# Weight sums of a seven-product scheme: three of four moved from VectorE to accumulating transfers issued by GpSimd

## The reference

```
xn   = rms_norm(h);  proj = xn @ w_in
h    = h + concat(gated_deltanet(...), moba_attention(...)) @ w_o
hn   = rms_norm(h)
h    = h + (silu(hn @ w_gate) * (hn @ w_up)) @ w_down        # w_gate, w_up: 2048 x 5632
gate = sigmoid(rms_norm(h) @ w_ple_gate)                     # 2048 x 2048
h    = h + gate * (p @ w_ple_proj)
```

## Time and profile before

| | |
|---|---|
| median of three runs | 1308.66 us (1308.38 to 1309.03) |
| span of the profiled execution, from its first to its last instruction | 1306.8 us |
| median of the runs above that span | 1.9 us |
| TensorE busy | 1299.9 us (99%) |
| VectorE busy | 1041.3 us (80%) |
| ScalarE busy | 710.7 us (54%) |
| GpSimd busy | 57.2 us (4%) |
| DMA | 238.37 MB, one queue for nearly all, 58.2% of 16 engines' span |

### The profile page before, as it was taken

One profiled execution on the slowest core, in us unless ns is written; L12 is line 12 of the kernel. 1 busy time (PEld: TensorE's weight loads), 2 busy tenths in 40 slices (PEclk: granted clock), 3 DMA queues, 4 the chain that ended last, 5 costly groups with the idle time before them and its releaser, 6 DMA issues.

```text
span 1306.8 us, 18407 instructions
## 1 busy us (share of the span) xinstructions
PE 1299.9 (99%) x6589; PEld 1074.1 (82%) x6589; DVE 1041.3 (80%) x1409; ACT 710.7 (54%) x946; POOL 57.2 (4%) x71
## 2 busy tenths in 40 slices
PE   9999999999999999999999999999999999999998
PEld 8788888888888888888888888888888888888887
DVE  6578885788586668999888978679888987968784
ACT  6576444544455556655555654445555555555653
POOL 5003000221000000000000000000000000000000
PEclk9999999999999999999999999999999999999999
DMA  8555554455444555665566656566666566556554
GB/s 272 178 176 162 160 147 129 146 147 148 145 127 145 178 176 161 215 219 181 188 198 205 204 187 215 182 211 188 195 205 214 181 189 210 190 178 224 178 179 163
DMA packets 126204, 238.37 MB, mean 182 GB/s; under 512 B 9711, under 2 KB 10786, under 8 KB 126138
## 3 DMA queue, kind: packets, MB, share of 16 engines
q1 hardware_dynamic: 126106, 237.48, 58.2%
q10 hardware_dynamic: 32, 0.01, 0.0%
HBM read 235.36 MB, written 2.10 MB: 182 GB/s over the span
## 4 chain that ended last, share of the span: by engine, by line
PE 97%; DVE 2%; ACT 0%; DMA 0%; issue 0%; DVEq 0%; ACTq 0%
PE pair L654 15%; PE pair L656 15%; PE pair L655 15%; PE pair L935 12%; PE pair L937 12%; PE pair L936 12%; PE bg L935 2%; PE bg L936 2%; PE bg L937 2%; PE bg L775 2%; PE bg L845 2%; PE bg L712 1%; PE bg L930 1%; DVE w_lo L1583 1%; PE bg L826 0%; PE bg L687 0%
## 5 line engine op out<-in xcount | busy, mean ns | idle before, releaser
L1583 DVE TENSOR_TENSOR w_lo<-raw,w_hi 128x1024 fp32r<-128x1024 f32 x442 | 533.1, 1222 | 160.7 <-ACT w_hi L1163 158.8
L1163 ACT ACTIVATE w_hi<-raw 128x1024 fp32r<-128x1024 f32 x399 | 416.4, 1056 | 254.6 <-PE pair L656 117.0
L654 PE MATMUL pair<-w_hi,xT_hi 128*128 128x512 f32 x716 | 289.7, 405 | 0.0
L656 PE MATMUL pair<-w_hi,xT_lo 128*128 128x512 f32 x716 | 279.9, 391 | 0.0
L655 PE MATMUL pair<-w_lo,xT_hi 128*128 128x512 f32 x716 | 279.4, 390 | 0.0
L656 PEld LDWEIGHTS pair<-w_hi,xT_lo 128*128 128x128 f32 x716 | 134.5, 188 | 29.1
L654 PEld LDWEIGHTS pair<-w_hi,xT_hi 128*128 128x128 f32 x716 | 134.7, 188 | 26.7 <-DVE w_lo L1583 0.3
L655 PEld LDWEIGHTS pair<-w_lo,xT_hi 128*128 128x128 f32 x716 | 134.9, 188 | 24.7
L1444 ACT ACTIVATE w_hi<-raw 128x1024 fp32r<-128x1024 f32 x43 | 45.7, 1063 | 141.5 <-DVE raw L1915 140.0
L935 PE MATMUL pair<-w_hi,actT_hi 128*128 128x512 f32 x296 | 115.7, 391 | 0.0
L937 PE MATMUL pair<-w_hi,actT_lo 128*128 128x512 f32 x296 | 115.2, 389 | 0.0
(11 more groups left out here) (386 smaller groups left out, 1959.8 us busy)
## 6 DMA issues: line engine op xcount, KB each, us to landing
raw<-in_w_in_dram SPq DMA_DIRECT2D x112, 512.0 KB, 3.8
raw<-in_w_gate_dram SPq DMA_DIRECT2D x88, 512.0 KB, 4.4
raw<-in_w_up_dram SPq DMA_DIRECT2D x88, 512.0 KB, 4.4
raw<-in_w_down_dram SPq DMA_DIRECT2D x88, 512.0 KB, 4.8
raw<-in_w_o_dram SPq DMA_DIRECT2D x32, 512.0 KB, 4.4
raw<-in_w_ple_gate_dram SPq DMA_DIRECT2D x32, 512.0 KB, 4.8
raw<-in_w_ple_proj_dram SPq DMA_DIRECT2D x4, 512.0 KB, 4.3
h<-in_x_dram SPq DMA_DIRECT2D x3, 512.0 KB, 7.8
```

The source lines that it names most:

```text
L654: mm(banks[t][:], hi[:, ts], wh, start=first, stop=False)
L656: m = mm(banks[t][:], lo[:, ts], wh, start=False, stop=last)
L1163: f(w_hi[j % RING][:], raw[j % RING][:], ACT.Copy).then_inc(hi_ready, 1)
L1583: v.tensor_tensor(w_lo[j % RING][:], raw[j % RING][:], w_hi[j % RING][:].bitcast(F32), ALU.subtract).then_inc(lo_ready, 1)
```

## The change

```
@gpsimd
+            def first_sum(u, j, n):
+                jg, ju = (j - 1) % RING, j % RING
+                pool.wait_ge(raw_landed[jg], (u - 1 - jg) * (16 // RING) + 16)
+                pool.wait_ge(raw_landed[ju], (u - ju) * (16 // RING) + 16)
+                g.dma_start(raw[ju][:, 0, :], raw[jg][:, 0, :], accum_op=ALU.add).then_inc(t1_ready, 16)
+                pool.wait_ge(lo_ready, u)
+                pool.wait_ge(t2_ready, n)
+                g.dma_start(raw[jg][:], t_raw[:, 0:1, :].to_broadcast([P, 2, CB]), accum_op=ALU.add).then_inc(t34_ready, 16)
...
+            def gate_up(i, u0, m0, seq, normed):
+                for q, m in enumerate(MIXED):
+                    j = seq.index(("up", m))
+                    first_sum(i * (2 * UPB) + (u0 + j), j, i * len(MIXED) + (m0 + q + 1))
+                    if normed and q == 1:
+                        norm(0)
...
@sync: three places like this one
-                            sp.wait_ge(t4_ready, i * len(MIXED) + (mg + MIXED.index(seq[j - RING][1]) + 1))
+                            sp.wait_ge(t_lo_ready, i * len(MIXED) + (mg + MIXED.index(seq[j - RING][1]) + 1))
...
@tensor: three places like this one
-                pe.wait_ge(t3_lo_ready, n)
-                product(bg[2][:], F_hi[:, q, 2, :], F_lo[:, q, 2, :], t_hi[:, 2, :], t_lo[:, 2, :], first, last)
-                pe.wait_ge(t24_lo_ready, n)
+                pe.wait_ge(t_lo_ready, n)
+                product(bg[2][:], F_hi[:, q, 2, :], F_lo[:, q, 2, :], t_hi[:, 1, :], t_lo[:, 1, :], first, last)
...
@scalar, split_mixed
-                act.wait_ge(t1_ready, n)
+                act.wait_ge(t1_ready, n * 16)
                 act.wait_ge(unit_used, u - (RING - 1))
                 f(w_hi[j % RING][:], raw[j % RING][:], ACT.Copy).then_inc(hi_ready, 1)
+                if between:
+                    between()
                 if not n0_first:
                     act.wait_ge(t_used, n - 1)
-                f(t_hi[:, 2, :], t3_raw[:], ACT.Copy).then_inc(t3_hi_ready, 1)
-                if between:
-                    between()
-                act.wait_ge(t4_ready, n)
-                f(t_hi[:, 0:2, :], t24_raw[:], ACT.Copy).then_inc(t24_hi_ready, 1)
+                act.wait_ge(t2_ready, n)
+                f(t_hi[:, 0, :], t_raw[:, 0, :], ACT.Copy).then_inc(t_hi_ready, 1)
+                act.wait_ge(t34_ready, n * 16)
+                f(t_hi[:, 1:3, :], raw[(j - 1) % RING][:], ACT.Copy).then_inc(t_hi_ready, 1)
...
@vector, split_mixed
                 dve.wait_ge(raw_landed[ju], (u - ju) * (16 // RING) + 16)
-                v.tensor_tensor(t3_raw[:], raw[ju][:, 1, :], raw[ju][:, 0, :], ALU.subtract).then_inc(t3_ready, 1)
-                dve.wait_ge(t3_ready, n)
-                v.tensor_tensor(raw[ju][:, 0, :], raw[ju][:, 0, :], raw[jg][:, 0, :], ALU.subtract).then_inc(t1_ready, 1)
-                dve.wait_ge(t1_ready, n)
-                v.tensor_tensor(t24_raw[:, 0, :], raw[ju][:, 1, :], raw[ju][:, 0, :], ALU.subtract).then_inc(t2_ready, 1)
-                dve.wait_ge(t2_ready, n)
-                v.tensor_tensor(t24_raw[:, 1, :], raw[jg][:, 1, :], t24_raw[:, 0, :], ALU.subtract).then_inc(t4_ready, 1)
+                dve.wait_ge(t1_ready, n * 16)
+                v.tensor_tensor(t_raw[:, 0, :], raw[ju][:, 1, :], raw[ju][:, 0, :], ALU.subtract).then_inc(t2_ready, 1)
                 split(u, j)
                 if between:
                     between()
-                dve.wait_ge(t3_hi_ready, n)
-                v.tensor_tensor(t_lo[:, 2, :], t3_raw[:], t_hi[:, 2, :].bitcast(F32), ALU.subtract).then_inc(t3_lo_ready, 1)
-                dve.wait_ge(t24_hi_ready, n)
-                v.tensor_tensor(t_lo[:, 0:2, :], t24_raw[:], t_hi[:, 0:2, :].bitcast(F32),
-                                ALU.subtract).then_inc(t24_lo_ready, 1)
+                dve.wait_ge(t_hi_ready, 2 * n - 1)
+                v.tensor_tensor(t_lo[:, 0, :], t_raw[:, 0, :], t_hi[:, 0, :].bitcast(F32), ALU.subtract)
+                dve.wait_ge(t_hi_ready, 2 * n)
+                v.tensor_tensor(t_lo[:, 1:3, :], raw[jg][:], t_hi[:, 1:3, :].bitcast(F32),
+                                ALU.subtract).then_inc(t_lo_ready, 1)
```

More of the change, by code:

```diff
@@ L636, in _, with norm @@
                         post(*s)
-            for i in range(2):
+            def norm(i):
                 pool.wait_ge(h_sum, i + 1)
                 rstd(h_rs[i][:], h_ms[i][:], h_s[i][:], 1.0 / D, EPS, h_rstd, i)
+            def first_sum(u, j, n):
[12 more added lines that the diff above has]
+                        norm(0)
+            for n, n0, ug, ud, mg, md in ((FF_A, 0, U_GUA, U_DA, MIX_GUA, MIX_DA), (FF_B, FF_A, U_GUB, U_DB, MIX_GUB, MIX_DB)):
+                for i in range(n):
+                    gate_up(i, ug, mg, SEQ if n0 or i else FIRST_SEQ, not (n0 or i))
+                seq, dm, _ = down_order(n)
+                for m in range(2):
+                    for q, k in enumerate(dm):
+                        j = m * len(seq) + seq.index((1, k))
+                        first_sum(ud + j, j, md + 2 * m + q + 1)
+            norm(1)
+            for q, m in enumerate(PG_MIXED):
+                j = PG_SEQ.index((1, m))
+                first_sum(U_PG + j, j, MIX_PG + q + 1)
         @block.tensor
@@ L1047, in down @@
                                     False).then_inc(unit_used, 1)
-                            pe.wait_ge(t3_lo_ready, count)
-                            product(bg[2][:], D_hi[:, q, 2, :], D_lo[:, q, 2, :], t_hi[:, 2, :], t_lo[:, 2, :], first, last)
-                            pe.wait_ge(t24_lo_ready, count)
+                            pe.wait_ge(t_lo_ready, count)
+                            product(bg[2][:], D_hi[:, q, 2, :], D_lo[:, q, 2, :], t_hi[:, 1, :], t_lo[:, 1, :], first, last)
                             product(bg[1][:], D_hi[:, q, 0, :], D_lo[:, q, 0, :], t_hi[:, 0, :], t_lo[:, 0, :], first, last)
-                            product(pair[0][1][:], actT_hi[:, k1, a1], actT_lo[:, k1, a1], t_hi[:, 1, :], t_lo[:, 1, :], False,
+                            product(pair[0][1][:], actT_hi[:, k1, a1], actT_lo[:, k1, a1], t_hi[:, 2, :], t_lo[:, 2, :], False,
                                     last).then_inc(t_used, 1)
@@ L1108, in _ @@
                             False).then_inc(unit_used, 1)
-                    pe.wait_ge(t3_lo_ready, MIX_PG + q + 1)
-                    product(bg[2][:], E_hi[:, q, 3, :], E_lo[:, q, 3, :], t_hi[:, 2, :], t_lo[:, 2, :], first, last)
-                    pe.wait_ge(t24_lo_ready, MIX_PG + q + 1)
+                    pe.wait_ge(t_lo_ready, MIX_PG + q + 1)
+                    product(bg[2][:], E_hi[:, q, 3, :], E_lo[:, q, 3, :], t_hi[:, 1, :], t_lo[:, 1, :], first, last)
                     product(bg[1][:], E_hi[:, q, 1, :], E_lo[:, q, 1, :], t_hi[:, 0, :], t_lo[:, 0, :], first, last)
-                    product(pair[0][1][:], xT_hi[:, k1, a1], xT_lo[:, k1, a1], t_hi[:, 1, :], t_lo[:, 1, :], False,
+                    product(pair[0][1][:], xT_hi[:, k1, a1], xT_lo[:, k1, a1], t_hi[:, 2, :], t_lo[:, 2, :], False,
                             last).then_inc(t_used, 1)
@@ L2022, in gate_up @@
                         dve.wait_ge(v_ready, i * 2 + (2 * n0 + 2))
-                        v.tensor_tensor(gate_s[1][:], pair[0][1][:], u_s[:], ALU.add).then_inc(gate_sum, 1)
+                        v.tensor_tensor(gate_s[1][:], pair[0][1][:], u_s[:], ALU.subtract).then_inc(gate_sum, 1)
                     if j == 2 * UPB - 1:
```

38 lines of the change are left out of this document (18 added, 20 removed).

## The result

The changed kernel takes 1637.9 us in the median (1630.5 to 1640.0) against 1308.8 before: a ratio of 1.250 (95% interval 1.248 to 1.253), 329 us slower. The forecast was 1531. Its mechanism is there, a loop through raw that TensorE has to wait for, and the bill is half as large again as I made it.

The account below looks back on a forecast made before the run. TensorE was taken as the bound, busy 1299.9 of 1306.8 us. Added stalls of 177 us in gate and up blocks, 33 in down and 12 in the last product make 222, so 1308.7 + 222 = 1531 us; range 1410 to 1690.

Parts of the forecast that it names:

- Nothing to win on VectorE: All 43 pairs: removing 89 us of VectorE instructions can shorten the time by no more than 0.9 us.
- The loop: From one t_lo to the next through raw: load, D1, t2, D2, rounding, rest; 15.9 us where TensorE wants 7.5.
- D1: Each pair's first adding transfer, 256 KB, before t1 can be rounded: taken as 4.1 us.
- D2: Each pair's second adding transfer, 512 KB, before t3 and t4 can be rounded: taken as 4.8 us.
- not slower: Rival: no stall if D1 + D2 stay under 1.3 us, time 1308 to 1310; chance 0.02.
- The stalls: TensorE waits for t_lo about twice in a block, 7.7 and 8.4 us, none at pair 1.
- my own sign that more than this loop is late: Stalls of TensorE at pair 1, or on ordinary units, would show this.
- The step that failed: After a block's third pair, loads catch up in about 22 us, so each of 11 blocks pays 16.1 anew, about 177.
- pair 1 late by 1.3 us: First pair of a down pass: t_lo expected at 786.8 against 785.52.
- A pass: Down: second pair's t_lo at 803.9 against 795.72, 8.2 us late; four passes, 33 us.
- The clock: Rival: TensorE's clock falls to 1.2 GHz in stalls, 33 us more, 1564; chance 0.2.
- Short and long transfers: Rivals on both transfers: short, 2.4 and 3.4 us, 1424, chance 0.18; long, 6.6 each, 1706, chance 0.15.

Follow-up runs that it names:

- Experiment 3: Changed kernel with GpSimd clearing an idle tile for about as long as the two transfers took, first, third and fourth sums left out: 1581.9 us, ratio 1.209.
- Experiment 1: Kernel before the change, all sums on VectorE, with only SP's three waits moved from the fourth sum to the rests: 1361.6 us, ratio 1.040.
- experiment 4: Changed kernel with TensorE multiplying zeros ahead of its waits to keep it busy: 1648.4 us, ratio 1.258.
- experiments 9 and 7: 9: changed kernel with spare up-unit tile, later rounding of third and fourth sums, first sum on VectorE, 1462.8 us; 7: same, first sum by transfer, 1527.0 us.
- experiment 10: Changed kernel with the first sum back on VectorE and TensorE multiplying zeros ahead of its waits for the rests: 1506.6 us, ratio 1.152.
- experiment 2: Changed kernel with only the first sum by transfer, VectorE making the others and the load waiting for the fourth sum: 1404.5 us, ratio 1.074.
- experiment 6: Changed kernel with the up units of pairs 2 and 3 in gate and up loaded into a spare tile: 1576.2 us, ratio 1.204.
- experiment 5: Changed kernel with the first sum given back to VectorE, only the third and fourth by transfer: 1525.2 us, ratio 1.166.

## Why the prediction was right, and where it was wrong

**Nothing to win on VectorE: right.** It lost 82.8 us of work, about the 89 forecast, and TensorE's end didn't depend on it.

**The loop, its place and its length: right.** A round was 15.9 by the sum and is 16.4; its terms load 3.7 (4.4), D1 4.1 (3.5), D2 4.8 (5.0, and 0.6 to hand over). In none of the 22 rounds does the chain that ended last, as the profile follows it back, go over TensorE. Experiment 3 makes the same loop without a transfer and loses 273 us. Experiment 1 shows that the later release costs by itself, with VectorE's own sums in the loop. The rival *not slower* needed D1 + D2 under 1.3 us; they are 8.5.

**The stalls: right in sum, not in place.** TensorE waits some 222 us, the forecast's 222, but that is chance. In a block the two parts at pair 2 are 7.9 (7.7 forecast) and at pair 3 6.2 (8.4 forecast), and the first of each is at the up unit, which I hadn't seen: D1 adds into it, so it too is late. And my own sign that more than this loop is late came: TensorE waits for t_lo at 40 of the 43 pairs, at pair 1 of the block shown for 0.97 us.

**The step that failed** is the one behind the third pair: "After it come four plain units and the next block's first four, about 22 us in which the loads catch up, as the chain of the next block starts from its own first units. So each block pays 16.1 anew." By that a block lasts 58.5 us, two rounds of 15.9 and a stretch of 26.7, in which TensorE goes at its pace. Measured it is 33.7 and 31.1, 64.8 us: the rounds are 1.9 of the difference, the stretch 4.4, and 11 times the sum of both is 69 of the 78 us by which the blocks were mis-sized. The loads don't catch up. The units behind pair 3 and the next block's first ones go through the same ring in SP's order, and pair 1's up unit is the eighth load after SP's wait; then come D1, second sum, D2, rounding and rest. That chain is as long as the stretch. The chain that ended last, as the profile of the changed kernel follows it back, has two forms there. One block (start, us, what):

```profile
620.53 3.68 DMA raw<-in_w_up_dram
...
633.28 5.23 DMA raw<-in_w_up_dram
...
639.04 3.60 DMA raw<-raw
```

and the next:

```profile
684.68 0.79 PE bg L965
...
700.08 0.24 PE pair L967
```

In five of the nine stretches it is the first: from SP's wait over loads, splits and the engines' work at the end of the block to pair 1's up unit and D1, with no product of TensorE in it. In three it is the second: 16 us of TensorE's products, the slow ones among them, and then VectorE's work at the end of the block. The ninth goes over 9.4 us of products and then the load and D1. From the second sum on all are alike: D2, rounding, rest. With the clock held the stretch grows to 32.2 us (experiment 4), and without D1 it shrinks by 2.2 (experiments 9 and 7). The second transfer is what keeps it long: where it is made, or a delay as long stands in its place, the stretch is 28.9 or more, in experiment 10 with the clock at 1.00; without it, it is 26.7, with the first transfer (experiment 2) and with none (experiment 1).

The second mis-sized term is D1 and D2 at one price each. In the changed kernel D2 took 5.0 us in 40 of the 43 pairs. D1 took 3.3 to 4.7 us from issue to landing in 35 pairs, and 4.3 to 6.8 in the eight in which SP issued a load within 0.8 us of it; three of these eight are the first pair of a pass of down. In the first pass it was issued at 912.32, between two loads, and the second sum came at 918.88, 6.6 us later. There I had pair 1 late by 1.3 us; TensorE waited 4.7. A pass costs 14.7 to 17.6 and not 8.2.

**The clock: the rival's mechanism came, its price didn't.** The granted clock fell to 0.84 over a block and 0.70 in its second round, and products behind stalls ran at the level of 1.2 GHz. In the half change this cost 18.5 us (experiment 10), where the rival had 33 for the whole. In the full change holding the clock won nothing (experiment 4: 10 us slower), but a longer first transfer came in its place, so what the slow products cost there isn't shown. The Trainium skill, TensorE: Matmul & The Clock Gate, Part 1, has the throttled clock as the default that activity lifts; the trace agrees, 1.00 before and 0.84 in a block with 15 us of stalls. That products are slow is one thing, that they are on the path another: in the changed kernel they are on it in four of the nine stretches and in none of the rounds.

**Short and long transfers: excluded by the table of transfers**, 3.9 and 5.0 us at the median. By the formula of the Trainium skill, DMA: Bandwidth & Descriptors, "Anatomy of one DMA", they would be 2.6 and 3.2 as an estimate; the measured ones are 1.3 and 1.8 us longer, for transfers that add.

**What stays open.** How the 4.4 us of the stretch divide between the lower clock and the chain of loads and transfers isn't shown. In the changed kernel the two forms are nearly equal, 30.1 to 30.6 us where TensorE's products lead and 30.5 to 30.8 in three of the five where the loads do (32.1 and 34.1 in the other two, each the first stretch of its stage), and in experiment 4 what took the slow products away made the first transfer longer. Nor was it tried why a load issued next to an adding transfer makes it longer, if it does.

## What to carry to other kernels

Ask of a transfer that replaces an instruction not what it frees but which loop it is in: here three VectorE instructions of 0.69 us, off the path, became 8.5 us of transfers in a loop that sets when the next load may start, and the time rose by 25%. Follow such a loop all the way round, past the stretch in which things "catch up", and charge a transfer at the price that it has with loads issued next to it. If a wait is only moved later, time that by itself first: here it cost 53 us without any transfer.

## What the runs showed of the hardware that I had not expected

- The time of an adding transfer went with what SP issued next to it. 256 KB, from issue to landing: in the changed kernel 3.3 to 4.7 us in the 35 pairs with no load issued within 0.9 us, 4.3 to 6.8 in the other eight; 5.3 and 6.7 in experiment 2 with a load 0.1 to 0.2 us ahead. 512 KB: 5.0 with none near, 6.3 with a load 1.2 us behind, 8.1 to 8.4 with two, 0.6 and 1.2 behind (experiment 6). It isn't all of it: two of 6.4 us (issued at 611.74 in the changed kernel, at 594.20 in experiment 5) had no load near. The DMA engines' share doesn't tell them apart: 0.82 in a transfer of 3.5 us, 0.71 in one of 5.3.
- In the changed kernel GpSimd is busy 0.91 us with the issue of the smaller one and 1.20 with the larger, and in the round shown 0.56 us pass between the end of the second sum and the start of that issue.
- Holding TensorE's granted clock at 0.989 instead of 0.919 by products of zeros changed the time by +10 us, in the wrong direction; at 1.00 instead of 0.949 in the half change it won 18.5.
